# Hybrid encoder block on eight cores: DMA transposes for the second tile, a 32-row short block, weights eight ahead, three copy buffers

## The reference

```
u = rms_norm(h, g_mix); z = u @ w_in               # value, gate, pool, gate A, gate B: 5 x 1024 columns
a = z_val * sigmoid(z_gate)
a = depthwise_conv(a, width 31) + b_dw             # along the tokens
y_conv = silu(layer_norm(a)) @ w_conv_out
y_pool = (per-group linear map of (window mean of p - p)) * scale @ w_pool_out    # windows 2, 4, 8, 16
h = h + (sigmoid(gA) * y_conv + sigmoid(gB) * y_pool) @ w_o
v = rms_norm(h, g_ffn)
h = h + (silu(v @ w_gate) * (v @ w_up)) @ w_down   # 2816 inner columns
out = rms_norm(h, g_final)
```

## Time and profile before

| | us |
|---|---|
| median of 3 runs (1049.71 to 1051.41) | 1050.55 |
| profiled execution | 1050.06 |
| its span, first to last instruction, slowest core (core 0) | 1048.5 |
| spans of the eight cores | 1043.0 to 1048.5 |
| TensorE busy | 1010.4 |
| VectorE, ScalarE, GpSimd busy | 429.1, 304.8, 176.1 |

### The profile page before, as it was taken

The page is one execution under the profiler, slowest core; times in us unless marked ns, Lnnn a source line. Parts: engine busy times, 40 slices in busy tenths (PEclk is TensorE's granted clock), DMA queues, the critical chain, the costliest instruction groups (busy, mean ns, idle before and its releaser), DMA issues.

```text
span 1048.5 us, 16942 instructions; the slowest of 8 cores (1043.0 to 1048.5 us)
## 1 busy us (share of the span) xinstructions
PE 1010.4 (96%) x5894; PEld 502.8 (48%) x5972; DVE 429.1 (41%) x630; ACT 304.8 (29%) x530; POOL 176.1 (17%) x329
## 2 busy tenths in 40 slices
PE   5889999999999999999999999999999999999996
PEld 2555555444454444444456565444445444444442
DVE  3464554742472322221244665574247222121133
ACT  2424354612152332221112334461215211111111
POOL 2511112011113121110222111101111311111001
PEclk8999999999999999999999999999999999999998
DMA  7899896363439656550839979326342955544022
GB/s 183 143 246 196 160 175 112 65 111 55 70 117 175 124 95 106 76 75 6 136 127 234 199 149 164 50 43 130 55 67 89 142 80 81 73 77 72 1 71 101
DMA packets 59381, 116.21 MB, mean 111 GB/s; under 512 B 9699, under 2 KB 9699, under 8 KB 59298
## 3 DMA queue, kind: packets, MB, share of 16 engines
q0 software_dynamic: 38592, 70.27, 44.7%
q1 hardware_dynamic: 18402, 36.72, 11.8%
q10 hardware_dynamic: 2304, 8.13, 1.9%
HBM read 159.72 MB, written 8.39 MB: 160 GB/s over the span
## 4 chain that ended last, share of the span: by engine, by line
PE 89%; SPq 4%; DMA 4%; issue 1%; DVE 1%; ACT 0%; DVEq 0%; POOLq 0%; POOL 0%; ACTq 0%
PE ps L374 84%; PE ps L499 5%; SPq L214 4%; DMA h<-xe 2%; DMA rep<-aT 1%; PE ps L406 1%; DVE ub L396 0%; ACT sqj L384 0%; DVEq L910 0%; DVE uT L415 0%; ACT uT L417 0%; ACT sqj L722 0%; DVE h L720 0%; DVE aT L468 0%; POOLq L910 0%
## 5 line engine op out<-in xcount | busy, mean ns | idle before, releaser
L374 PE MATMUL ps<-vT,wr 128*128 128x512 bf16 x1378 | 304.5, 379 | 1.6
L374 PE MATMUL ps<-uT,wr 128*128 128x352 bf16 (+2 forms) x1648 | 291.4, 334 | 9.6 <-DVE uT L415 8.5
L214 POOL DMA_DIRECT2D wr<-wst x268 | 142.9, 537 | 700.0 <-PE ps L374 631.2
L374 PEld LDWEIGHTS ps<-uT,wr 128*128 128x128 bf16 x1664 | 162.0, 98 | 135.2 <-issue 19.2
L374 PEld LDWEIGHTS ps<-vT,wr 128*128 128x128 bf16 x1408 | 137.1, 98 | 162.6
L374 PE MATMUL ps<-wr,fT 128*128 128x512 bf16 x690 | 151.5, 379 | 0.7
L702 DVE TENSOR_TENSOR fT<-ps,sgf 128x512 bf16<-128x512 f32 x88 | 60.8, 691 | 221.1 <-PE ps L374 196.3
L701 ACT ACTIVATE sgf<-ps 128x512 f32<-128x512 f32 x88 | 52.5, 597 | 218.3 <-PE ps L374 218.3
L374 PEld LDWEIGHTS ps<-wr,fT 128*128 128x128 bf16 x704 | 68.9, 98 | 83.0
L499 PE MATMUL ps<-rep,wr 128*32 128x512 bf16 x1024 | 59.9, 388 | 7.3 <-DMA rep<-aT 7.3
L722 ACT ACTIVATE sqj<-h 128x512 bf16<-128x512 f32 x32 | 20.1, 630 | 134.0 <-DVE h L720 128.9
(11 more groups left out here) (70 smaller groups left out, 658.6 us busy)
## 6 DMA issues: line engine op xcount, KB each, us to landing
wr<-wst POOLq DMA_DIRECT2D x268, 256.0 KB, 5.1
rep<-aT SPq DMA_DIRECT2D x256, 65.8 KB, 4.7
xt<-xe SPq DMA_DIRECT2D x24, 512.0 KB, 3.7
out<-h ACTq DMA_DIRECT2D x15, 512.0 KB, 2.7
h<-xe SPq DMA_DIRECT2D x8, 512.0 KB, 6.4
wpt<-wpt SPq DMA_DIRECT2D x4, 256.0 KB, 7.0
gb_s<-gb SPq DMA_DIRECT2D x2, 512.0 KB, 7.6
out<-h ACTq DMA_DIRECT2D x1, 256.0 KB, 2.1
```

What stands on the lines that cost most here:

```text
L214: e.dma_start(out=o[1], in_=o[2]).then_inc(o[3], 16)
L374: S.op(PE, lambda e: e.matmul(out, lhsT=lhsT, rhs=rhs, start=start, stop=stop), [lhsT, rhs], [out], signal=signal)
```

## The change

Four things, in one edit. The short row block is loaded and normalised with 32 rows in place of 31 (a 32nd row is added to the input on the host; in tile 0 only the load has 32 rows). The row blocks of tile 1 are transposed by DMAs that SyncE issues, from `ub` straight into `uT`, without TensorE, PSUM and the eviction. `rel` puts out loads only up to eight units ahead of the one taken last, until convolution 3 of tile 0, and up to the ring's size after that. A third buffer `rep` lies over the memory of `ub`, and the copies of every group are issued as soon as its values are there.

```diff
-XROWS = TOK + 2 * HALO + 1
+XROWS = TOK + 2 * HALO + 2
...
-    rep = [m1.get(f"rep{i}", [128, 4, EXTP], BF16) for i in range(2)]
+    m1d = Area(ub_start, ub_start + NUB * 2048 + 2048)
+    rep = [(m1 if i < 2 else m1d).get(f"rep{i}", [128, 4, EXTP], BF16) for i in range(3)]
...
+    tr_sem = [Prod(sem(f"d_tr{i}"), 16) for i in range(2)]
...
-    wstate = {"next": 0, "li": 0, "freed": 0}
+    wstate = {"next": 0, "li": 0, "freed": 0, "lead": 8}
...
     def rel(k=1):
         wstate["freed"] += k
-        prefetch(k + 1)
+        room = wstate["li"] + wstate["lead"] - wstate["next"]
+        if room > 0:
+            prefetch(min(room, k + 1))
...
+    def xbar_transpose(rec, dsem, out_ap, in_ap):
+        rg, wg = S._sets([in_ap], [out_ap], (), ())
+        S._waits(rec, S._deps(rg, wg, dsem, dsem.count + 16))
+        dsem.count += 16
+        rec.ops.append(("ins", lambda e: e.dma_start_transpose(out_ap, in_ap).then_inc(dsem.sem, 16), False))
...
         xbuf[(i, idx)] = buf
+        n = (n + 15) // 16 * 16
         S.dma(SP, sm, buf[0:n, :], xe.ap()[row0:row0 + n, :])
...
     def s0_chain(i, idx):
         r, n = SUBS[idx]
+        n = (n + 15) // 16 * 16
         norm_chain(xbuf[(i, idx)][0:n, :], n, 0, idx % NUB)
 
-    def s0_transpose(i, idx, eng=None):
+    def s0_transpose(i, idx):
         r, n = SUBS[idx]
-        norm_transpose(n, uT, r, idx % NUB, eng)
+        n = (n + 15) // 16 * 16
+        xbar_transpose(SP, tr_sem[idx % 2], uT[:, :, r:r + n], ub[idx % NUB][0:n, :])
...
     def im2col(c):
-        st = c % 2
+        st = c % 3
...
     def vg_done(c):
         rel(2)
-        if c < 2:
-            im2col(c)
+        im2col(c)
...
         rel(1)
-        if c + 2 < KC:
-            im2col(c + 2)
...
+            if i == 0 and st == "c3":
+                wstate["lead"] = RING
```

## The result

The changed kernel takes 1040.01 us in the median, beside 1050.86 for the kernel before: a ratio of 0.9895, 95% interval 0.9875 to 0.9914, or 10.9 us less. The forecast was 1037.3, its range 1031 to 1042. The profiled execution took 1040.15 us.

What follows compares the result with a forecast made beforehand. TensorE, busy 96%, was taken as the bound, its start held up by a 31-row load on one DMA engine. With core 6 ending last, 35.3 + 1003.9 - 4.0 + 1.6 + 0.5 = 1037.3 us; range 1031 to 1042.

Steps and rivals of the forecast that it cites:

- the start: Up to T8, the start's last transpose: matmuls start at 18.4, not 25.30; T8 at 35.3, not 43.27; 8.0 us gained.
- the third buffer: Tile 1's last convolution: the 2.29 us wait for shifted copies goes on core 0; tile 0's waits stay.
- the sum: Core 6 to the end: 35.3 + 1003.9 - 4.0 = 1035.2 of span, plus 1.6 and 0.5: 1037.3 us.
- a sign of being wrong: At the start: the prediction is wrong if the wait there only changes its name.
- The bound of 5.7: Start's lowest gain: clock low all the same and the weight 1.2 us later, T8 at 37.6.
- The transposes: Tile 0's feed-forward stage: 152.8 us becomes 148.8, 4.0 us gained; the DMA transposes replacing TensorE's cost 0.
- The bounds of 2.7 to 13.8 us for one: One 256 KB DMA transpose: like four 32-partition copies, 2.7 us, or like the lone engine, 13.8; nothing lost at either.
- the slower rival: Tile 0's feed-forward stage: DMA transposes hold all engines and weight loads fall behind; at 20 us each, 1088; chance 0.05.
- Weights eight ahead: GpSimd's weight loads: the limit leaves the order of that stream as it is; no effect in either direction.
- The rival with the convolutions' waits gone, 1031: Tile 0's convolutions: the limit of eight thins out the burst, core 6 loses its 6.3 us of waits; chance 0.13.
- the cover of 2.0 us: Tile 1's last convolution: copies land at 654.1, TensorE arrives at 656.1.
- the forecast's 1035.2: Span at the end of core 6, taken to end last: 35.3 + 1003.9 - 4.0.

Runs made afterwards that it cites:

- The triple transposes: The changed kernel with each DMA transpose of tile 1's rows issued three times, one after the other: 1041.3 us in a single execution.
- the three kernels with held loads: Changed kernel, GpSimd waiting for TensorE before further weight loads: 1036.24 us; also value matmuls before gate matmuls: 1035.57; also two pooling-weight loads moved later: 1034.23.

## Why the prediction came out as it did

The sign, the range and the cause of the two large parts held; the time came out 2.7 us above the forecast. The terms that were mis-sized are the start, the clock behind it (no term at all) and the third buffer.

**The start: cause right, size 1.0 us too large, and part of it given back.** The loads of 31 rows and of 32, and the one split in two, show that the single 31-row load held up the later ones. T8 moved by 7.0 us on core 0 (43.27 to 36.28) where the sum had 8.0. I had bounded the start of the matmuls by the first weight, 18.4 against 18.60 measured, but kept the steps behind it as they were. The next weight became late there, 2.54 us at 25.16: in that part the wait only changed its name, which the prediction had listed as a sign of being wrong. The bound of 5.7 allowed for loads 6 and 7 competing with the first weight, not for a second one. Block 3's load landed 10.2 us after its issue, not within 8; that was soon enough. Stretches of the changed kernel, columns as in the earlier trace rows:

```profile
16.00:20.40 4.40, 2.41 (x26) 1.83 (x27) 2.41 (x5) 1.55 (x4) 1.10 (x3) 1.00 0.96 214
20.40:25.00 4.60, 1.80 (x16) 1.03 (x14) 3.45 (x5) 2.44 (x5) 1.63 (x4) 1.00 1.01 292
...
37.20:40.60 3.40, 3.40 (x13) 1.71 (x14) 0.25 (x1) 0.46 (x1) 2.92 (x6) 0.51 1.17 135
40.60:58.00 17.40, 17.40 (x117) 11.27 (x115) 9.71 (x14) 4.18 (x9) 3.71 (x7) 1.00 1.07 206
```

The hole from 21.5 to 22.9, one engine of sixteen, is gone: the engines' share is 0.96 and 1.01 up to 25. That the last waits are for loads that stand behind others in that stream is argued from this and not tested.

Of the 7.0 us, 4.65 reach the second convolution. The sum had let all of it through. From 37.2 to 40.6 the granted clock was 0.51, the lower of its two levels, while TensorE worked without a gap: the 128 matmuls took 20.93 us where the same ones took 19.25 in the kernel before, 1.7 us. The other 0.8 is the first convolution's longer wait (1.79 against 1.02), as its copies moved forward by less than T8 did. No step of the prediction had a term for the clock after the start. Nor did it see that the second convolution runs at the lower clock before the change too, so that its wait of 4.02 us is not all that it loses there; the earlier trace rows show the row cut off by the window, this is the whole of it:

```profile
79.35 5.32 PE L499 MATMUL ps<-rep,wr 128*32 128x512 bf16 x64 [4.02 <-DMA rep<-aT]
```

On core 0 this is the same 5.32 us before and after, so it moves nothing in the sum; six cores have it before and all eight after.

**The transposes: right to a tenth.** 152.8 to 148.8, as read off the two tiles' stages. The bounds of 2.7 to 13.8 us for one held. Transposes of tile 1's rows, duration on SyncE and time to landing:

```profile
L427 SPq DMA_TRANSPOSE uT<-ub x9: 1177/1239/1517, 331.9 to 442.3; - x9
...
DMA to landing us min/median/max: 2.7/3.8/6.6
```

The DMA engines' share in that stage rose from 0.55 to 0.64 over the same 345 to 480 us. The triple transposes show that the slower rival was further off than the prediction could know. Against the figures from the Trainium skill ("VectorE: DVE Perf Modes", section "The three transpose paths"): 72 TensorE transposes cost 4.0 us here, 55 ns each among other matmuls, not 390, and a block of eight came by DMA in 3.8 us in the median, not in the 10.5 that eight times the page's 1309 ns would make, an estimate.

**Weights eight ahead: right, nothing.** GpSimd's burst is the same 13 loads, at 33.19 in place of 40.17:

```profile
33.19 6.93 POOL L214 DMA_DIRECT2D wr<-wst  x13
```

The limit counts what is recorded, not what has run, so it holds nothing back. The rival with the convolutions' waits gone, 1031, needed it to bind; made to bind, it is worth 4.9 us, where the rival had put 6.3, for the waits alone; some 1.7 of the 4.9 are the clock in the second convolution.

**The third buffer: place right, size too large.** The wait of 2.29 us became 0.85 on core 0 instead of nothing. Tile 1 runs 8.6 us earlier by then (4.65 + 4.0), so the prediction's last issue of group 7's copies, 649.4, becomes 640.8, and its landing, 654.1, becomes 645.5. The issue came at 642.1, the landing at 648.17; from issue to landing the set took

```profile
DMA to landing us min/median/max: 5.1/5.8/6.8
```

and not the 4.7 of the sum. TensorE would have begun at 647.68 (648.53 - 0.85), so the cover of 2.0 us was used up, half by the issue and half by the landing. The profile names a ScalarE instruction for the wait, which ended 0.12 us after that landing. But on the other seven cores the same convolution starts before that instruction does, so it does not need it: what it waited for is the copies. In time the part is not measurable: without the third buffer two cores wait a third time for copies, with it one (core 0), and the core that ends last is not always one of these.

**Which core ends last.** The prediction let core 6 set the end; in the profiled execution it is core 0 (1038.6, core 6 has 1036.2). Core 0 lost 1.7 us to the clock from 37.2 on and kept 0.85 us of its third wait. Core 6 ran that stretch at full clock, but lost some 1.5 us earlier, from 24.8 to 30.5, where its granted clock was 0.70; its T8 came at 37.36, 2.1 us after the forecast's 35.3. Against that its second convolution waited 3.08 us in place of 4.67, a wait that the forecast had left as it was. So that core 6 ends only 1.0 us after the forecast's 1035.2 is in part luck: two misses of opposite sign.

**The sum in measured terms,** core 0: 1048.5 - 7.0 + 1.7 + 0.8 - 0.1 - 4.0 - 1.3 = 1038.6, where 0.1 is the second convolution coming a little sooner after the first.

## What to carry to other kernels

A load that goes through one engine, as the 31 rows did, costs most for what is queued behind it: look in the stretches for a short time in which one engine of sixteen works, and count in what is late next, and next after that. A limit on how far ahead loads are put out holds only if the issuing engine waits for something; counted while the program is recorded, it changed nothing here. A wait of the matmul engine can cost more than its length: look whether what follows it runs at the lower clock. Where the program runs the same stage with and without an operation, the difference of the two is its price, better than any figure for the operation by itself.

## What the runs showed of the hardware

In the changed kernel the granted clock fell to its lower level on cores 0 to 3 for some 3.4 us, beginning between 36 and 38 us, with TensorE fully busy in it; from 30.0 to 36.4 us TensorE of core 0 had been busy for 4.34 us, at full clock. Cores 4, 6 and 7 had such a stretch earlier (mean granted clock 0.83 to 0.90 from 20 to 30 us). In the kernel before, seven of the eight cores passed the same place at full clock, as core 0 does here:

```profile
44.20:47.60 3.40, 3.40 (x24) 2.22 (x25) 0.76 (x2) 0.46 (x1) 3.24 (x7) 1.00 1.06 139
```

On all eight cores of the changed kernel, and on six before, it fell again in tile 0's second convolution, behind a wait for copies of 3.1 to 4.8 us: 5.1 to 6.5 us in place of 3.64. In the three kernels with held loads no convolution of tile 0's first two that had not waited ran slow, and not every one that had waited did: cores 3 and 7 of the kernel before waited 3.46 and 3.26 us and took 3.64. Why the clock falls on some cores and not on others is open.

DMA transposes of 128x1024 16-bit numbers took 1.2 to 1.5 us of SyncE each to issue, and landed in 2.7 to 6.6 us beside running weight loads; three in a row held SyncE for 11.5 to 19.4 us, and 27 of them in one feed-forward stage left its 148.8 us as they were.
